# Gate scalings placed between normalised tiles, eight result buffers, and a gate multiplied ahead of its norm

## What is computed

```
# layer 0: two groups of four heads, from one input projection
oB = _rmsnorm(oB, p['ret_norm'][a]) * jax.nn.silu(hd(bg, B_HEADS))
mix = jnp.concatenate([oA.reshape(B, T, A_VW), oB.reshape(B, T, B_VW)], axis=-1)
x = x + mix @ p['w_out0'][a]
# layer 1: up-projection of the normalised x into 16 tiles xm and 16 tiles zg
h = _rmsnorm(x, p['norm_mix'][l])
xm, zg = jnp.split(h @ p['w_up1'][c], 2, axis=-1)
# ... causal convolution of xm, q/k/v, matrix memory, giving hC
x = x + (hC * jax.nn.silu(zg)) @ p['w_down1'][c]
# after each mixer a SwiGLU feed-forward; at the end
y = _rmsnorm(x, p['norm_final'])
```

## Time and profile before

| | |
|---|---|
| time, median of 3 runs | 2135.77 us (2133.35 to 2139.61) |
| the profiled execution's own time | 2138.1 us |
| its span, first to last instruction | 2136.3 us |
| mean granted clock of TensorE | 0.979 of full speed |
| busy: PE, its weight loads, DVE, ACT, POOL | 2047.6, 1871.6, 1047.9, 428.8, 895.3 us |

### The profile page before, as it was taken

One profiled execution on the slowest core, in us unless ns is written; L12 is line 12 of the kernel. 1 busy time (PEld: TensorE's weight loads), 2 busy tenths in 40 slices (PEclk: granted clock), 3 DMA queues, 4 the chain that ended last, 5 costly groups with the idle time before them and its releaser, 6 DMA issues.

```text
span 2136.3 us, 33690 instructions
## 1 busy us (share of the span) xinstructions
PE 2047.6 (96%) x13453; PEld 1871.6 (88%) x13453; DVE 1047.9 (49%) x1230; ACT 428.8 (20%) x671; POOL 895.3 (42%) x568
## 2 busy tenths in 40 slices
PE   6999999899999999989999999999899999999997
PEld 5989988799999999989998746547499999999996
DVE  4655646554415414576962356555732441442345
ACT  3232333321101100131212323323211110010011
POOL 4323333145445445554553123223445444544543
PEclk9999999899999999999999999999999999999998
DMA  4122212122222222233232474756732222222222
GB/s 174 60 70 78 85 54 91 42 69 70 78 79 70 79 79 70 88 108 127 79 103 77 144 259 146 275 191 208 282 104 74 71 76 79 69 79 72 76 79 89
DMA packets 82080, 224.49 MB, mean 105 GB/s; under 512 B 6352, under 2 KB 11344, under 8 KB 81232
## 3 DMA queue, kind: packets, MB, share of 16 engines
q1 hardware_dynamic: 73344, 202.94, 28.7%
q10 hardware_dynamic: 8656, 20.39, 2.6%
HBM read 170.06 MB, written 53.25 MB: 105 GB/s over the span
## 4 chain that ended last, share of the span: by engine, by line
PE 85%; DVE 8%; DMA 3%; ACT 2%; issue 1%; POOL 1%; DVEq 0%; SPq 0%; ACTq 0%; POOLq 0%
PE psd L211 12%; PE psd L216 11%; PE psd L212 11%; PE psd L215 11%; PE psd L217 11%; PE psd L218 11%; PE psm L429 2%; PE psm L1397 1%; PE psd L1293 1%; DMA c_s<-CsB 1%; PE psd L1282 1%; PE psd L1219 1%; DMA CsB<-st_c 1%; PE psm L1382 1%; DVE ntmp L306 1%
## 5 line engine op out<-in xcount | busy, mean ns | idle before, releaser
L1986 POOL CAST whi<-wraw 128x1024 fp32r<-128x1024 f32 x223 | 236.7, 1062 | 935.2 <-PE psd L218 501.9
L1988 POOL TENSOR_TENSOR wlo<-wraw,whi 128x1024 fp32r<-128x1024 f32 x223 | 543.9, 2439 | 17.9
L211 PE MATMUL psd<-xh,whi 128*128 128x320 f32 x896 | 286.3, 320 | 9.6 <-ACT xh L269 3.5
L215 PE MATMUL psd<-xl,whi 128*128 128x320 f32 x896 | 279.6, 312 | 2.7 <-POOL xl L324 2.2
L211 PE MATMUL psd<-ah,whi 128*128 128x320 f32 x864 | 269.2, 312 | 12.1 <-DVE ffs L974 7.7
L212 PE MATMUL psd<-xh,whi 128*128 128x320 f32 x896 | 278.8, 311 | 0.0
L216 PE MATMUL psd<-xl,whi 128*128 128x320 f32 x896 | 278.7, 311 | 0.0
L218 PE MATMUL psd<-xh,wlo 128*128 128x320 f32 x896 | 278.6, 311 | 0.0
L217 PE MATMUL psd<-xh,wlo 128*128 128x320 f32 x896 | 278.6, 311 | 0.0
L212 PE MATMUL psd<-ah,whi 128*128 128x320 f32 x864 | 267.9, 310 | 0.0
L216 PE MATMUL psd<-al,whi 128*128 128x320 f32 x864 | 267.8, 310 | 0.0
(11 more groups left out here) (396 smaller groups left out, 3225.2 us busy)
## 6 DMA issues: line engine op xcount, KB each, us to landing
wraw<-w SPq DMA_DIRECT2D x224, 512.0 KB, 3.5
CsA<-st_c SPq DMA_DIRECT2D x7, 1024.0 KB, 6.3
CsB<-st_c SPq DMA_DIRECT2D x7, 1024.0 KB, 9.1
c_s<-CsA SPq DMA_DIRECT2D x7, 1024.0 KB, 6.5
c_s<-CsB SPq DMA_DIRECT2D x7, 1024.0 KB, 9.4
ztp<-st_c SPq DMA_DIRECT2D x5, 1024.0 KB, 8.4
CsC<-st_c SPq DMA_DIRECT2D x5, 1024.0 KB, 9.4
c_s<-ztp SPq DMA_DIRECT2D x5, 1024.0 KB, 4.2
```

What stands on the lines that cost most here:

```text
L211: pe.matmul(o0, wh, x0, start=st, stop=False)
L215: pe.matmul(o0, wh, l0, start=False, stop=False)
L1986: pool.tensor_copy(whi[s][:], wraw[s][:]).then_inc(w_high, 1)
L1988: pool.tensor_tensor(wlo[s][:], wraw[s][:], whi[s][:].bitcast(F32), ALU.subtract).then_inc(w_split, 1)
```

## The change

Three things change, in DVE's, ACT's and SP's programs. PE and POOL have the same instructions in the same order as before.

1. In the up-projection of layer 1, DVE scales gate unit 1 behind normalised tile 3, gate unit 2 behind tile 6, and gate unit 3 behind tile 7 as before. ACT makes Silu and stores in the same places; only gate unit 3 stays behind the store of `xT` and the four loads.
2. The final norm's eight result tiles have a buffer each: the four `ntmp` and the four tiles `ffs` and `fft`. The waits for `y_stored` within the loop are gone.
3. `b_vec_mix` first multiplies `b_t` by the gain and the gate `z_bg`, as soon as ACT has squared `b_t`, and then by the norm's factor `b_k`.

```
-                        buf = ntmp[k % 2 if self.final else k % 4]
-                        if k >= 2 and self.final:
-                            v.wait_ge(y_stored[k % 2], 16 * (k // 2))
-                        elif k >= 4:
+                        buf = yt[k] if self.final else ntmp[k % 4]
+                        if k >= 4 and not self.final:
                             v.wait_ge(*self.ready(k - 4))
...
-            v.wait_ge(bS.sem, bS.at("r", h))
-            v.scalar_tensor_tensor(gb["t"][:], gb["t"][:], par[:, PAR["ret"]:PAR["ret"] + 1], gb["k"][:], ALU.mult,
+            v.wait_ge(bS.sem, bS.at("sq", h))
+            v.wait_ge(z_done.sem, z_done.at("bg", h))
+            v.scalar_tensor_tensor(gb["t"][:], gb["t"][:], par[:, PAR["ret"]:PAR["ret"] + 1], zbg[:], ALU.mult,
                                    ALU.mult).then_inc(bV.sem, 1)
             v.wait_ge(bV.sem, bV.at("mixn", h))
-            v.wait_ge(z_done.sem, z_done.at("bg", h))
-            v.tensor_tensor(mix[:, bass.ds(h + 4, 1), :].rearrange("p a c -> p (a c)"), gb["t"][:], zbg[:],
+            v.wait_ge(bS.sem, bS.at("r", h))
+            v.tensor_tensor(mix[:, bass.ds(h + 4, 1), :].rearrange("p a c -> p (a c)"), gb["t"][:], gb["k"][:],
                             ALU.mult).then_inc(bV.sem, 1)
...
                 norm2.high(a, [0])
                 self.raw_gate(a, 0)
-                norm2.high(a, range(1, KD))
+                norm2.high(a, range(1, 4))
+                self.raw_gate(a, 1)
+                norm2.high(a, range(4, 7))
+                self.raw_gate(a, 2)
+                norm2.high(a, [7])
...
-                for j in range(1, Z_RAW):
-                    self.raw_gate(a, j)
+                self.raw_gate(a, 3)
...
-                sp.dma_start(io["yT"][:, k, :], ntmp[k % 2][:]).then_inc(y_stored[k % 2], 16)
+                sp.dma_start(io["yT"][:, k, :], yt[k][:]).then_inc(y_stored[k % 2], 16)
```

More of the change, by code:

```diff
@@ L161, in trunk @@
         fft = [sb(f"fft{s}", [P, T], at=n0) for s in range(2)]
+        yt = ntmp + ffs + fft
         psd = [ctx.enter_context(nc.psum_tensor(f"psd{s}", [P, 2, 512], F32)) for s in range(2)]
@@ L1090, in vec @@
                 self.raw_gate_scaled(v, 0)
[L1091 to L1094, removed]
+                norm2.scaled(v, range(1, 4))
+                self.raw_gate_scaled(v, 1)
+                norm2.scaled(v, range(4, 7))
+                self.raw_gate_scaled(v, 2)
+                norm2.scaled(v, [7])
+                norm2.low(v, 7)
+                self.raw_gate_scaled(v, 3)
                 v.wait_ge(self.w_in, 64)
```

## The result

The changed kernel takes 2123.05 us (median of 5 runs, 2119.52 to 2123.36) beside 2136.91 us for the kernel before (5 runs, 2133.35 to 2141.08). The ratio, taken over all runs and not from the two medians, is 0.9928, with a 95% interval from 0.9917 to 0.9939: 13.0 to 17.7 us less (13.9 between the medians). The prediction said 2120.6 and 15.2 us less.

What follows compares the result with a forecast made beforehand. PE, busy for 96% of the span, was taken as the bound. Terms 10.1 + 0.9 + 4.2 = 15.2 us, taken from the median 2135.8, gave 2120.6 us, with a range of 2116.5 to 2127.5.

Steps and rivals of the forecast that it cites:

- The gates: Layer 1's up-projection: moving the gate scalings removes PE's pause before gate unit 3 and the slow unit behind it, 10.1 us.
- I cost the moved scalings at nothing: DVE in the up-projection: the two moved scalings lie in time DVE lost anyway, so they cost 0 us.
- The room at x unit 2: Up-projection: ACT takes the first x unit out by 967.8, 3.7 us before PE needs its pair at 971.5.
- The rival of the burst: Up-projection: last gate's store takes 9.8 us, PE waits 1.8 and loses 2.4 to half clock; price 4.2 us, chance 0.07.
- The gate ahead of the norm: Last head of layer 0: one DVE multiplication instead of two after the norm's factor, so PE's pause shrinks, 0.9 us.
- bounds of 0 to 3.3: End of layer 0: gain nothing if half clock eats it, 3.3 us if the shorter pause saves a slow stretch.
- The result's buffers: Final norm: eight result tiles run in a row on DVE without waiting for stores, 4.2 us gained.
- alternative sum: Final norm at about 358 GB/s: 0.915 us a tile, a gain of 3.8, total 14.8 in place of 15.2 us.
- The range's 3.8: Final norm: the gain of 3.8 us from the result's buffers used for the low end of the range of gains.
- Given back: End of the up-projection: something other than PE sets it, the 10.1 us become a wait, 5.1 us left, 2130.7; chance 0.05.
- More half clock: Where PE is the bound: half-clock time after waits doubles, costing up to 25 us, 2145; chance 0.02.

## Why the prediction came out right

**The gates, 10.1 us.** Measured in the trace 10.0 us, 9.5 with the gates alone. The method, from matmul to matmul against the step of a dense stretch, gave the size; PE's idle time alone (7.74 us) would have missed the slow unit. "I cost the moved scalings at nothing" holds to 0.1 us. That 10.1 was met so closely is in part chance, since the old pause cost 9.8 to 10.5 from trace to trace.

**The room at x unit 2, 3.7 us.** This step failed; by luck it changed the sum little. The prediction let the last gate's store land 4.3 us after its issue, the median of three stores of before. Its issue came as forecast (959.66 + 3.01 = 962.67 in the time of before, forecast 962.70), but it took 7.6 us, over even the slowest of the three:

```profile
DMA to landing us min/median/max: 2.2/4.3/4.8
```

These 3.3 us more were most of the room, and ACT's issue of `wgx` ahead of the x unit, which the forecast left out, took the other 0.4. In before, SP issued no load of weights between 955.36 and 971.65, because PE's pause held the splits back. Now it issued one at 958.47, ahead of the store, and one at 965.53: the DMA engines moved 326 GB/s over the 14 us from 953, that is 4.6 MB, beside 361 GB/s over 11 us from 956, 4.0 MB. That this sharing is the cause is argued from these sums. That a longer burst ahead delays the store is shown by the store made twice, with which it landed 7.3 us later in the time of before: ACT could issue it only at 964.66, and it took 8.8 us from there. Such a delay would have cost over 9 us; here the store landed just in time.

The rival of the burst had the right mechanism with too long a landing (9.8 us); it took 0.16 us here and 0.6 in three other kernels. Its price of 4.2 us added 2.4 us of half clock to a pause of 1.8 us; no run has such a pause here, and the one of 3.22 us brought none.

**The gate ahead of the norm, 0.9 us.** The pause shrank by 0.85 us, as computed. The times say 1.5 to 2.1, inside the bounds of 0 to 3.3; the upper bound was there because the half clock might fall better, which it did in most traces with this part.

**The result's buffers, 4.2 us.** 4.3 in the trace, 4.9 (3.0 to 6.8) alone. The stores moved 394 GB/s over four microseconds in the middle of the row. The figure of some 358 GB/s in the Trainium skill, page DMA: Bandwidth & Descriptors, section Specifications, by which the prediction's alternative sum was 14.8, is exceeded here. The range's 3.8 for this term rested on that figure too. The rate read from the rows, 380, was the nearer one.

**The rivals.** Given back: PE's waits between 930 and 1130 us hold one row in the changed kernel, 0.8 us for ACT's `pre`, and a row of 0.8 for it stands before as well, there behind 1130 us; the ruler reads 13.01 and 13.02 at both ends. More half clock: the clock from 1178 to 1540 us is 0.96 as in the earlier trace rows, and 0.89 instead of 0.84 from 366 to 430.

**The time.** 2120.6 was the sum taken from the median of three runs; 2123.05 lies 2.4 above, within the range. The three terms are met to 0.2 us in the trace, so what is left is the spread of whole runs: of the 18.6 us between the two profiled executions 3.4 belong to no term. The 1.2 of them ahead of PE's pause at 411 us are half clock (a mean of 0.83 in before and 0.91 in the changed kernel from the split at 366 to that at 416 us); for the rest no cause is shown.

## What to carry to other kernels

Where PE waits for a buffer that a small operation of another engine frees, move that operation ahead of the long ones in front of it, and cost the pause from matmul to matmul, since slow matmuls behind the pause may go with it. Then follow the transfers that ran while the pause held other loads back: a landing time read from before can be too short (4.3 us became 7.6 here), and whatever PE needs should not stand behind a wait for such a landing. Before giving a loop more buffers, divide the landing time by the time of a step: 2.4 us is three tiles of 0.81, so with the one being written four buffers do.

## What the runs showed of the hardware

- A DMA's issue itself can take long behind a large one on the same engine's queue. Behind the store of 2560 KB in the changed kernel ACT's issues of `wqkv` and `gsm` take 1.35 and 1.41 us, where that of the store itself took 0.33. Behind two such stores, in ACT's timeline of the kernel with the store made twice:

```profile
953.60 1.22 ACTq L993 DMA_DIRECT2D cst<-conv  x1
954.85 5.96 ACTq L994 DMA_DIRECT2D wqkv<-wqkv  x1
960.84 1.68 ACTq L995 DMA_DIRECT2D gsm<-gsm  x1
```

  These issues held the last gate's store back as well: it was issued at 964.66, though DVE's scaling for it had ended at 953.52 + 0.83 = 954.35.
- Between 370 and 388 us the same code ran at half clock for the whole of the stretch or for about half of it, and from the split at 366 to that at 416 us this moves the time by 1.2 to 1.5 us (48.2 us with the gates alone, 49.4 in before, 49.7 in the changed kernel without `b_vec_mix`). From 1163 us to the end of layer 1's heads the profiled kernels differ by 3.8 us (from 2.25 lost to 1.6 gained against before), with no difference in the code there. A term of under 2 us can't be read from the time of one run here, but it can be read from the trace at its place.
- DVE's scaling that reads PSUM and one SBUF tile took 0.81 us beside POOL's cast (at 941.47) and beside POOL's subtraction (at 949.90), where operations on two SBUF tiles took up to 3.02 us beside the subtraction.
